# Where 106 weight chunks lie in their slots: 96 or 160 bytes in, instead of 64

## The reference

```python
# first block
h = rmsnorm(x, norm1_g); u, v_a, q, k, v_b = split(h @ w_in)
y_a = chunked_spatial_gating(u, v_a, ...); y_b = rmsnorm(diff_attention(q, k, v_b, ...))
g_a, g_b = split(sigmoid(h @ w_gate + b_gate))
x = x + (g_a * (y_a @ w_up_a) + g_b * (y_b @ w_up_b)) @ w_out
x = x + hierarchical_moe(rmsnorm(x, norm2_g), ...)      # 32 experts, top 2
# second block, two layers, on x and on 256 context tokens
for layer in range(2):
    x, ctx = (s + 0.5 * gate * swiglu(modulate(rms_norm(s), ...), ffn1) for s in (x, ctx))
    x = x + gate * merge_mixers(attention(x with ctx), pooling, fft, w_out)
    x = x + 0.5 * gate * swiglu(modulate(rms_norm(x), ...), ffn2)
    # ctx goes through the same mixers and ffn2 in the first layer only
return rms_norm(x) * final_gain
```

## Time and profile before

| what | value |
|---|---|
| median of 3 runs | 2116.39 us (2115.34 to 2120.51) |
| the profiled execution | 2116.8 us, of which span 2115.1 us |
| PE busy | 2028.8 us (96%) |
| PEld busy | 1713.3 us (81%) |
| DVE / ACT / POOL busy | 1396.8 / 677.1 / 245.3 us |
| chain that ended last | PE 83%, DVE 7%, DMA 6%, ACT 2%, issue 1% |
| granted TensorE clock | 0.989 of full speed over the span |

### The profile page before, as it was taken

How to read it: one execution, slowest core, us unless ns; L and a number is a source line. 1 busy time by engine, 2 the same in 40 slices (tenths; PEclk the granted TensorE clock), 3 DMA queues, 4 the chain that set the end, 5 groups by cost and what they waited for, 6 DMA issues and landing times.

```text
span 2115.1 us, 32243 instructions
## 1 busy us (share of the span) xinstructions
PE 2028.8 (96%) x13718; PEld 1713.3 (81%) x13718; DVE 1396.8 (66%) x1826; ACT 677.1 (32%) x918; POOL 245.3 (12%) x286
## 2 busy tenths in 40 slices
PE   8999988987999999999999999999999999989998
PEld 7988985554888888886798888889888888868998
DVE  6887553333888599356579668737866874666565
ACT  6554321111412212245532112124211212464343
POOL 1000002231101010400121000031100104001000
PEclk9999999899999999999999999999999999999999
DMA  9656769999666565332136466434645644315674
GB/s 281 214 173 204 238 255 390 407 412 405 202 186 181 159 196 160 113 100 66 41 100 199 139 170 179 127 110 147 197 140 165 181 137 122 120 46 159 179 198 123
DMA packets 384124, 387.19 MB, mean 183 GB/s; under 512 B 18041, under 2 KB 351342, under 8 KB 371566
## 3 DMA queue, kind: packets, MB, share of 16 engines
q1 hardware_dynamic: 355438, 304.31, 44.8%
q0 software_dynamic: 27952, 79.77, 12.2%
q10 hardware_dynamic: 592, 1.05, 0.1%
HBM read 430.68 MB, written 1.05 MB: 204 GB/s over the span
## 4 chain that ended last, share of the span: by engine, by line
PE 83%; DVE 7%; DMA 6%; ACT 2%; issue 1%; SPq 0%; POOL 0%; DVEq 0%; POOLq 0%; ACTq 0%
PE B L2037 25%; PE B L2039 24%; PE B L2038 24%; DMA WB<-in_w 5%; PE B L2497 3%; PE B L2867 1%; DVE HF L1241 1%; PE B L2532 1%; DMA W<-in_w 1%; PE B L2841 1%; PE B L2852 1%; DVE hL L1229 1%; DMA WB<-in_w,ROWS 0%; DVE LO0S L847 0%; DVE R L858 0%
## 5 line engine op out<-in xcount | busy, mean ns | idle before, releaser
L2037 PE MATMUL B<-hH,HI 128*128 128x512 f32 x992 | 388.2, 391 | 0.8 <-DVE LO L847 0.8
L2039 PE MATMUL B<-hH,LO 128*128 128x512 f32 x992 | 386.2, 389 | 0.0
L2038 PE MATMUL B<-hL,HI 128*128 128x512 f32 x992 | 385.9, 389 | 0.0
L935 DVE SCALAR_TENSOR_TENSOR MACC<-MADW,CS,MACC 128x1024 f32<-128x1024 f32 x224 | 277.4, 1279 | 7.9 <-DMA MADW<-in_ada_w 2.6
L1596 ACT ACTIVATE HI<-RAW 128x2048 fp32r<-128x2048 f32 (+3 forms) x112 | 181.6, 1621 | 199.7 <-PE B L2039 160.5
L1819 ACT ACTIVATE T<-B 128x512 f32<-128x512 f32 (+1 forms) x88 | 48.0, 545 | 599.0 <-PE B L2039 598.9
L847 DVE TENSOR_TENSOR LO<-RAW,HI 128x2048 fp32r<-128x2048 f32 (+3 forms) x112 | 215.0, 1919 | 16.1 <-ACT HI L1596 12.8
L2037 PEld LDWEIGHTS B<-hH,HI 128*128 128x128 f32 x992 | 186.2, 188 | 39.8 <-DVE LO L847 1.0
L2039 PEld LDWEIGHTS B<-hH,LO 128*128 128x128 f32 x992 | 186.2, 188 | 39.1
L2038 PEld LDWEIGHTS B<-hL,HI 128*128 128x128 f32 x992 | 186.3, 188 | 38.1
L1332 DVE SCALAR_TENSOR_TENSOR XC<-B,MOD,XC 128x256 f32<-128x256 f32 x136 | 60.7, 479 | 197.1 <-PE B L2039 196.9
(11 more groups left out here) (516 smaller groups left out, 4742.1 us busy)
## 6 DMA issues: line engine op xcount, KB each, us to landing
MADW<-in_ada_w POOLq DMA_DIRECT2D x128, 512.0 KB, 3.9
RAW<-in_ffn_w_gu SPq DMA_DIRECT2D x120, 512.0 KB, 5.5
W<-in_w SPq DMA_DIRECT2D x31, 1024.0 KB
WB<-in_w SPq DMA_DIRECT2D x28, 1024.0 KB
WA<-in_w SPq DMA_DIRECT2D x17, 1024.0 KB
RAW<-in_ffn_w_down SPq DMA_DIRECT2D x36, 384.0 KB, 3.8
RAW<-in_ffn_w_down SPq DMA_DIRECT2D x36, 320.0 KB, 4.4
WAHEAD<-in_w SPq DMA_DIRECT2D x11, 1024.0 KB, 17.1
```

What stands on the lines that cost most here:

```text
L935: ins = V.scalar_tensor_tensor(MACC[:, v, :], MADW[n % 2][:], c, MACC[:, v, :], ALU.mult, ALU.add)
L2037: mm(o, wh, xh, start=first, stop=False, **more)
L2038: mm(o, wh, xl, start=False, stop=False, **more)
L2039: return mm(o, wl, xh, start=False, stop=last, **more)
```

## The change

`BY_HALVES` becomes 96 bytes into the slot. A third place, `AS_ROWS`, 160 bytes in, is given to the 12 chunks that are the moving operand. WHOLE stays at 0. The tiles of the three places are named "", "S" and "R". Nothing else changes: on every engine the same instructions with the same waits stand in the same order, and only the addresses of 106 chunks differ. The address of what is loaded minus that of what moves, modulo 256, becomes 96 for stationary chunks, and minus 160, that is 96 as well, for moving ones.

```diff
-BY_HALVES, WHOLE = (LINE, LINE), (0, 0)
+BY_HALVES, WHOLE, AS_ROWS = (LINE + 32, LINE + 32), (0, 0), (3 * LINE - 32, 3 * LINE - 32)
...
-    places = [BY_HALVES] * FIRST_CHUNKS
+    places = [BY_HALVES] * 8 + [AS_ROWS] * 8 + [BY_HALVES] * (FIRST_CHUNKS - 16)
...
-    places += [BY_HALVES] * 2 + [WHOLE] + [BY_HALVES] * 2
+    places += [BY_HALVES] * 2 + [WHOLE] + [AS_ROWS] * 2
...
-    places += [BY_HALVES] * 4 + [WHOLE]
+    places += [BY_HALVES] * 2 + [AS_ROWS] * 2 + [WHOLE]
...
-            return {place: nc.alloc_sbuf_tensor_at(f"{name}{i}" if place == 0 else f"{name}{i}S", [P, CHUNK], dt,
-                                                   offset=at0 + place) for place in (0, LINE)}
+            return {place: nc.alloc_sbuf_tensor_at(f"{name}{i}{tag}", [P, CHUNK], dt, offset=at0 + place)
+                    for place, tag in ((0, ""), (LINE + 32, "S"), (3 * LINE - 32, "R"))}
```

More of the change, by code:

```diff
@@ L328, in build @@
         FW = at(69, "FW", [P, LAYERS, 2, S])
-        assert union + 1024 * 83 + LINE <= nc.sbuf_usable_end, (union + 1024 * 83 + LINE - nc.sbuf_usable_end)
+        assert union + 1024 * 83 + 3 * LINE <= nc.sbuf_usable_end, (union + 1024 * 83 + 3 * LINE - nc.sbuf_usable_end)
         h_at = [base + 4 * KT * 2 * S * i for i in (1, 2)]
```

## The result

The changed kernel took 2128.18 us (median of 6 runs, 2126.84 to 2131.26) against 2116.70 for the kernel before (6 runs, 2115.34 to 2120.51): a ratio of 1.0055, 95% interval 1.0046 to 1.0065. I had forecast 2108 us, and the range ended at 2123. The change costs 11.5 us by the medians and 12.9 us in the profiled executions (span 2128.0 against 2115.1).

The account below looks back on a forecast made before the run. PE, busy 96% of the span, was taken to bound the kernel. Long steps turned short gave 10.3 - 0.5 - 1.0 - 0.3 = 8.5 us; 2116.8 - 8.5 = 2108.3, stated as 2108 us, range 2104 to 2123.

Parts of the forecast that it names:

- PE sets the pace: Nearly everywhere a BY_HALVES chunk is used, PE (busy 96%) bounds; 256-column matmuls start every 117.8 ns (long) or 113.3 ns (short).
- The share of short steps: 256-column matmuls: short-step share near 0 at distance 0, 58% at 64, 27% at 192; same slope gives 87% at 96.
- all long steps become short, minus 10.3 us: PE, 106 chunks at distance 96: every long step of 256-column matmuls becomes short, 4.5 ns each, minus 10.3 us.
- Its upper bound: PE, 106 chunks at distance 96: at worst all steps take 120 ns, as at L2426, plus 24.7 us.
- What of it counts: Of 10.3 us, 0.5 hidden by DVE waits, 1.0 by experts' loads in flight, 0.3 behind pauses; 8.5 us left.
- ACT, DVE, DMA at nothing: Splits on ACT and DVE (0 to 1.1 us) and DMA landings (at most plus 1 us) were taken as 0.
- Rival 1: 256-column matmuls: each pause draws the long or short step whatever the distance; 2116 us, from 2111 to 2121; chance 0.23.
- Rival 2: Weight loads beside 256-column matmuls: dependence may repeat every 128 or 64 bytes; 2129 us at 117.8 ns, 2141 at 120; chance 0.21.
- Its other half: Part of Rival 2: an operand starting in the middle of a 64-byte line touches one line more; no separate size.

## Why the prediction was wrong, point by point

- *PE sets the pace where these chunks are used, and two steps exist, 117.8 and 113.3 ns.* Held for the kernel before. The result is found in the steps, 14.0 us of them for 12.9 us at the end, but the steps at 96 are of a third kind (115 to 122 ns).
- *The share of short steps rises away from 0 on both sides, 96 lies 32 bytes further out than 64, hence 87% short or more.* This is the step that failed. I drew one hump through two points (64 and 192) and a zero, and carried its slope on. That 192, as far from 256 as 64 is from 0, had half the share of 64 already spoke against a curve by distance alone. And that 32 bytes more would be a margin against being thrown out at a pause had no row behind it. The runs show two narrow good places, 64 and 192. At 96 3 of 5,260 steps are short; the term "all long steps become short, minus 10.3 us" was plus 14.0.
- *Its upper bound.* I had plus 24.7 us, with all steps at 120 ns. Measured: 118.0. The bound held, the choice within it did not, and the range, which ended at 2123 us, left most of that side out. Rows at 64, 192 and 0 said nothing of what lies between them.
- *What of it counts.* I took 1.8 us off 10.3. Of 14.0 us 12.9 arrived in the profile, 11.5 in the medians; where the rest went was not followed up.
- *ACT, DVE, DMA at nothing.* Held: 1913 and 2289 ns, 5.0 and 5.1 us to land. The rule of the Trainium skill (DMA: Bandwidth & Descriptors, section "How a descriptor splits into AXI transactions") on transfers that start off a 256-byte boundary showed nothing here either. It speaks of bytes fetched, and what moved here is where a chunk is written to.
- *Rival 1, the step is drawn at each pause whatever the distance.* Half true. At 64 it is drawn (494 against 515 matmuls in the same window and place), and runs of the kernel before spread by a standard deviation of 2.6 us (13 runs) and 2.4 us (17 runs), the 2.4 us that I had worked out for such draws; at 0, 96 and 128 the short step isn't among what is drawn. The independent read ports that the Trainium skill gives PE (SBUF — State Buffer, section "Who interferes with whom") do not make addresses free: only places changed between runs at 2112 and 2131 us.
- *Rival 2, the dependence repeats every 128 bytes, at 96 all at 117.8 ns, 2129 us.* The time came true (2128.2), and so did that 96 loses where 64 doesn't. I had given it 0.21, and argued against it with the difference of 0 and 64, which excludes a period of 64 but not of 128. Its mechanism came true in part: the short step stands at 64 and 192, 128 apart, but other places 128 apart differ (32 and 160, 80 and 208), and the steps at 96 are not the 117.8 ns that it priced, but five different ones with nearly the same mean. That the sum fits to 1 us is luck. Its other half, that a start in the middle of a 64-byte line costs, is excluded by the shift of everything.

What stays open is why 64 and 192 are good, why the order (64, 192) is better than (192, 64), why the steps elsewhere repeat every fourth, fifth or sixth matmul, and what draws the step after a pause. That the two reads of PE get in each other's way is my reading; the traces show the steps, not the meeting.

## What to carry to other kernels

Where weight loads of 128 columns run beside matmuls of 256, as here, the distance of their addresses modulo 256 was worth 4 to 6% of the step (113.3 ns against 118.0 at 96 and 119.9 at 160); scan it in one run by giving each chunk another place, before choosing one for all. Try high and low parts at different good places: (64, 192) was the best here. A mean can agree with a theory while the single steps do not, so read the steps too. A curve known at two points and a zero isn't known between them, least of all where the address decides: the range of a forecast from it should reach as far as the worst row's price.

## What the runs showed of the hardware

Products in fp32r with 256 moving columns and stationary chunks, mean step in ns and share of short ones by distance (64, 96 and 128 from whole kernels, the others from scans of one execution): 0: 119.7, 1%; 16: 118.6, 1%; 32: 118.3, 0; 48: 117.8, 0; 64: 115.2, 58%; 80: 118.7, 0; 96: 118.0, 0; 112: 119.9, 14%; 128: 118.9, 1%; 144: 118.3, 1%; 160: 119.9, 0; 176: 118.1, 1%; 192: 114.8, 66%; 208: 116.8, 0; 224: 116.8, 18%. The 512-column products at distance 0 keep 227 ns, twice the short step for twice the columns: at 0, where 256 columns lose, they don't. Other distances were not tried for them. Moving all addresses by 32 bytes changed nothing (1.0004).
